# The second expert table's product turned round: 128 tokens held and 512 table columns passing, with sums kept by token and no finishing stage

## The reference, cut to what matters

```python
def one_block(xb):                      # 128 tokens
    ...                                 # eidx: 8 heads x 16 experts of 16384, gate: their softmax
    u = u_tab[eidx]
    act = gelu(einsum('thkd,td->thk', u, xb))
    return einsum('thk,thkd->td', gate * act, v_tab[eidx])
y = rmsnorm(x + out, w_norm_final)
```

## Time and profile before

| what | value |
|---|---|
| median of 3 runs | 3663.56 us (3657.59 to 3664.55) |
| the profiled execution's own time | 3668.83 us |
| its span, first to last instruction | 3667.0 us, mean granted clock 0.984 |
| first matmul of `outputs` | 2554.84 us |
| PE / DVE busy from 3200 to 3400 us | 200.0 / 180.0 of 200 us |
| DMA moved in that stretch | 362 GB/s, share 0.91 |

### The profile page before, as it was taken

One profiled execution on the slowest core, in us unless ns is written; L12 is line 12 of the kernel. 1 busy time (PEld: TensorE's weight loads), 2 busy tenths in 40 slices (PEclk: granted clock), 3 DMA queues, 4 the chain that ended last, 5 costly groups with the idle time before them and its releaser, 6 DMA issues. The chain is left out here.

```text
span 3667.0 us, 50045 instructions
## 1 busy us (share of the span) xinstructions
PE 3528.2 (96%) x19463; PEld 3267.5 (89%) x19463; DVE 2585.5 (71%) x3886; ACT 1314.1 (36%) x1671; POOL 937.1 (26%) x619
## 2 busy tenths in 40 slices
PE   8999999998989999999999999998999999999996
PEld 6877777776867889999999999998999999999996
DVE  4135555553224238999998888886898898998997
ACT  5111134442223223332236767673222222222222
POOL 0000000000000000233333333331555554554552
PEclk9999999999999999999999999999999999999998
DMA  5145343435334244688789999998989999989896
GB/s 204 50 144 172 108 140 128 125 130 185 141 107 162 86 156 160 256 329 333 293 321 364 384 376 375 382 374 343 360 339 372 360 356 377 360 355 370 348 359 243
DMA packets 193659, 965.07 MB, mean 263 GB/s; under 512 B 19697, under 2 KB 67121, under 8 KB 92706
## 3 DMA queue, kind: packets, MB, share of 16 engines
q1 hardware_dynamic: 121010, 516.50, 37.9%
q0 software_dynamic: 61424, 426.27, 29.9%
q10 hardware_dynamic: 11008, 19.26, 1.5%
HBM read 865.58 MB, written 96.37 MB: 262 GB/s over the span
## 5 line engine op out<-in xcount | busy, mean ns | idle before, releaser
L2068 PE MATMUL hidden_hp<-dense_hi,whi 128*128 128x384 f32 x2048 | 699.8, 342 | 6.1 <-PEq L123 6.1
L1836 ACT CAST whi<-raw 128x2048 fp32r<-128x2048 f32 x214 | 410.7, 1919 | 790.5 <-PE outputs_vp L2559 599.9
L2069 PE MATMUL hidden_hp<-dense_lo,whi 128*128 128x384 f32 x2048 | 691.8, 338 | 0.0
L2557 PE MATMUL outputs_vp<-outputs_w_hi,whi 128*128 128x384 f32 x2032 | 679.6, 334 | 3.3 <-DVE wlo L1840 3.1
L2559 PE MATMUL outputs_vp<-outputs_w_hi,wlo 128*128 128x384 f32 x2032 | 678.8, 334 | 0.0
L2558 PE MATMUL outputs_vp<-outputs_w_lo,whi 128*128 128x384 f32 x2032 | 678.7, 334 | 0.0
L2015 POOL DMA_INDIRECT hidden_row<-u_rows,expert_ids x192 | 363.5, 1893 | 1000.4 <-DVE dots L2300 625.4
L1840 DVE TENSOR_TENSOR wlo<-raw,whi 128x2048 fp32r<-128x2048 f32 x214 | 490.2, 2291 | 105.0 <-ACT whi L1836 103.4
L2493 DVE SCALAR_TENSOR_TENSOR accg<-outputs_row,outputs_w_op,accg 128x2048 f32<-128x2048 f32 x192 | 450.7, 2347 | 54.8 <-DMA outputs_row<-v_rows,outputs_id 51.8
L2300 DVE CUSTOM_DVE_ANT_0 hidden_row<-hidden_row,hidden_h_row 128x2048 f32<-128x2048 f32 x192 | 436.0, 2287 | 67.7 <-DMA hidden_row<-u_rows,expert_ids 64.8
L2355 POOL DMA_INDIRECT outputs_row<-v_rows,outputs_id x192 | 325.6, 1696 | 522.3 <-DVE accg L2493 477.8
(11 more groups left out here) (397 smaller groups left out, 5032.6 us busy)
## 6 DMA issues: line engine op xcount, KB each, us to landing
raw<-v_units SPq DMA_DIRECT2D x128, 1024.0 KB
raw<-u_units SPq DMA_DIRECT2D x86, 1024.0 KB
raw<-w_in SPq DMA_DIRECT2D x42, 1024.0 KB, 5.8
hidden_raw<-u_units SPq DMA_DIRECT2D x42, 1024.0 KB
hidden<-hidden_hid SPq DMA_DIRECT2D x128, 192.0 KB
gate_mat<-units_big SPq DMA_DIRECT2D x12, 2048.0 KB, 20.0
units_big<-hidden SPq DMA_DIRECT2D x16, 1536.0 KB
units_big<-gate_mat SPq DMA_DIRECT2D x16, 1536.0 KB
```

What stands on the lines that cost most here:

```text
L1836: self.nc.scalar.copy(self.hi[s][:], self.raw[raw][:]).then_inc(self.hi_done, 1)
L2068: mm(o, un.hi[s][:, x, :], h_hi[:, x, :], start=x == 0, stop=False)
L2069: mm(o, un.hi[s][:, x, :], h_lo[:, x, :], start=False, stop=False)
L2557: mm(o, un.hi[x][:, at, :], W_hi[s][:, e, :], start=e == 0, stop=False)
```

## The change

The product is turned round: the held operand is now a 128-token block of the weights (`W_hi` or `W_lo`, [128 experts x 128 tokens]) and 512 table columns of `hi` or `lo` pass. v_tab's units are packed anew on the host: a unit is now 512 table columns of half a chunk's experts (4 x 128), so two units make one block q of 512 columns. A unit has 3 token tiles x 4 expert blocks x 3 products = 36 matmuls of 512 columns. Results are token by table column, so `acc` is three tiles [128 x 2048] that SP loads with the residual at the start of the stage; DVE adds three 128 x 512 banks every second unit. Six banks are used, two blocks q ahead. Chunk c's first unit needs only the first half of the chunk's `W_lo`. In the last chunk the gathered rows are taken one unit sooner. There is no `finish`: its norm, scaling and stores stand at the end of `outputs`, in a different order, one 1/sqrt for the three dense tiles together, with no transposes and no barrier between.

The core of the diff:

```diff
-                        add(i, s, j, 0)
-                        for x in range(3 * (DS * s + j) // 2, 3 * (DS * s + j + 1) // 2):
+                        for x in rows_of(i, s, j):
                             gathered(i, x)
-                        add(i, s, j, 1)
+            def add(c, q, first=False):
+                for t in range(DTILES):
+                    k = DTILES * (QB * c + q) + t
+                    vec.wait_ge(un.done, NKEYS + DTILES * (DS * c + 2 * q + 1) + t + 1)
+                    if first:
+                        vec.wait_ge(sums_in, 16 * TILES)
...
+                    o = acc[t][:, NB * q:NB * (q + 1)]
+                    v.tensor_tensor(o, o, vp[DTILES * (q % 2) + t][:], ALU.add).then_inc(added, 1)
...
+            for t in range(DTILES):
+                sp.dma_start(acc[t][:], sums[(t + 1) * P:(t + 2) * P, :]).then_inc(sums_in, 16)
             turns(sp, body, T)
...
+                        if j > 0 and j % 2 == 0:
+                            add(c, j // 2 - 1, isinstance(i, int) and i == s == 0)
+                        if j == 0 and not (isinstance(i, int) and i == s == 0):
+                            add(c - 1, QB - 1, isinstance(i, int) and i == 0 and s == 1)
...
+            for c in range(NCH):
+                s = c % 2
+                for j in range(DS):
+                    n, (q, h), x = DS * c + j, divmod(j, 2), j % 2
+                    if j < 2:
+                        pe.wait_ge(w_lo_done, 2 * c + j + 1)
+                    un.ready(pe, NKEYS + n)
+                    for t in range(DTILES):
+                        if h == 0:
+                            wait(pe, added, DTILES * (QB * c + q - 2) + t + 1)
+                        o, at = vp[DTILES * (q % 2) + t], slice(t * P, (t + 1) * P)
+                        for k in range(HC):
+                            e = HC * h + k
+                            mm(o[:], W_hi[s][:, e, at], hi[x][:, k, :], start=e == 0, stop=False)
+                            mm(o[:], W_lo[s][:, e, at], hi[x][:, k, :], start=False, stop=False)
+                            ins = mm(o[:], W_hi[s][:, e, at], lo[x][:, k, :], start=False, stop=e == CH - 1)
+                        ins.then_inc(un.done, 1)
...
-            sp.dma_start(X[:], sums[P:2 * P, :]).then_inc(early, 16)
-            sp.wait_ge(early, 16)
+            sp.wait_ge(gat.row_used, NGATHER - 2)
+            sp.dma_start(norm_w[:], w_row.partition_broadcast(P)).then_inc(norm_in, 16)
```

More of the change, by code:

```diff
@@ L2376, in outputs @@
         Gc = big[1][:, 0:CH * ND].rearrange("p (g e t) -> p g e t", e=CH, t=GT)
+        junk, half, norm_w = big[0][:, 0:D], big[1][0:NSMP, 0:D], gat.row[0]
         W_hi = [a.sb(f"w_hi{s}", [P, CH, ND], F32R) for s in range(2)]
@@ L2447, in body, with square, roots @@
                             weights_hi(2 * i + s + 1, 1 - s, (j - 4) // 2)
+            def square(x, to):
+                R, cols = x.shape[0], x.shape[1]
+                return nc.scalar.activation(junk[0:R, 0:cols], x, ACT.Square, accum_out=to)
+            def roots(n, rows, at):
+                act.wait_ge(meaned, n)
+                nc.scalar.activation(root[0:rows, at], mean[0:rows, at], ACT.Sqrt).then_inc(rooted, 1)
             weights_hi(0, 0, 0)
@@ L2451, in _ @@
             turns(act, body, T)
+            act.wait_ge(w_lo_done, 2 * NCH)
+            act.wait_ge(gat.row_used, NGATHER)
+            square(accg[0][:], ss[:, 0:1]).then_inc(squared, 1)
+            nc.scalar.copy(half, accg[1][NSMP:P, :]).then_inc(moved, 1)
+            roots(1, P, slice(0, 1))
+            act.wait_ge(added, DTILES * (QB * NCH - 1))
+            act.wait_ge(squared, 1)
+            for t in range(DTILES):
+                square(acc[t][:, 0:D - NB], part[:, t:t + 1]).then_inc(parts_done, 1)
+                act.wait_ge(parts_done, t + 1)
+            act.wait_ge(summed, 1)
+            square(accg[1][0:NSMP, :], ss[0:NSMP, 1:2]).then_inc(squared, 1)
+            act.wait_ge(squared, 2)
+            roots(2, NSMP, slice(1, 2))
+            for t in range(DTILES):
+                act.wait_ge(added, DTILES * (QB * NCH - 1) + t + 1)
+                square(acc[t][:, D - NB:D], ss[:, 2 + t:3 + t]).then_inc(squared, 1)
+                act.wait_ge(squared, 3 + t)
+            roots(3, P, slice(2, TILES))
         @block.vector
         def _(vec):
-            v = nc.vector
+            v, d = nc.vector, Steps(vec, dstep)
             def weigh(c, e):
@@ L2470, in weights_lo @@
                                 ALU.subtract).then_inc(w_lo_done, 1)
[L2472 to L2482, removed]
+            def add(c, q, first=False):
+                for t in range(DTILES):
+                    k = DTILES * (QB * c + q) + t
+                    vec.wait_ge(un.done, NKEYS + DTILES * (DS * c + 2 * q + 1) + t + 1)
+                    if first:
+                        vec.wait_ge(sums_in, 16 * TILES)
+                    else:
+                        wait(vec, added, k + 1 - DTILES * QB)
+                    o = acc[t][:, NB * q:NB * (q + 1)]
+                    v.tensor_tensor(o, o, vp[DTILES * (q % 2) + t][:], ALU.add).then_inc(added, 1)
             def gathered(i, j):
@@ L2493, in gathered, with rsqrt, scale @@
                 v.scalar_tensor_tensor(o[:], r[:], w_op[:, j:j + 1], o[:], mult, ALU.add).then_inc(gat.row_used, 1)
+            def rsqrt(n, rows, at):
+                v.tensor_scalar(mean[0:rows, at], ss[0:rows, at], 1.0 / D, EPS, mult, ALU.add).then_inc(meaned, 1)
+                vec.wait_ge(meaned, n)
+                vec.wait_ge(rooted, n)
+                newton_rsqrt(nc, d, rstd[0:rows, at], mean[0:rows, at], root[0:rows, at], tmp[0:rows, at])
+            def scale(x, n):
+                R = x.shape[0]
+                v.scalar_tensor_tensor(x, x, rstd[0:R, n:n + 1], norm_w[0:R, :], mult, mult).then_inc(done, 1)
             def body(i):
@@ L2519, in _ @@
             turns(vec, body, T)
+            vec.wait_ge(squared, 1)
+            rsqrt(1, P, slice(0, 1))
+            vec.wait_ge(norm_in, 16)
+            scale(accg[0][:], 0)
+            vec.wait_ge(moved, 1)
+            v.tensor_tensor(accg[1][0:NSMP, :], accg[1][0:NSMP, :], half, ALU.add).then_inc(summed, 1)
+            add(NCH - 1, QB - 1)
+            vec.wait_ge(squared, 2)
+            rsqrt(2, NSMP, slice(1, 2))
+            scale(accg[1][0:NSMP, :], 1)
+            vec.wait_ge(squared, TILES)
+            vec.wait_ge(parts_done, DTILES)
+            d(v.tensor_tensor(ss[:, 2:TILES], ss[:, 2:TILES], part[:], ALU.add))
+            d.wait()
+            rsqrt(3, P, slice(2, TILES))
+            for t in range(DTILES):
+                scale(acc[t][:], 2 + t)
         @block.tensor
@@ L2523, in _ @@
             mm = nc.tensor.matmul
[L2525 to L2560, removed]
```

128 lines of the change are left out of this document (34 added, 94 removed).

## The result

The change is slower: 3681.3 us, median of five runs (3676.0 to 3691.5), against 3664.6 (3657.6 to 3665.5), a ratio of 1.0049 with a 95% interval of 1.0035 to 1.0063. I had forecast 3640 and a gain of 23 us, and given 0.04 to a kernel slower than 3671. The profiled execution took 3685.5 us, its span is 3683.6.

A forecast was written before the change was run, and what follows sets the result against it. PE's matmul pace was taken as the bound, DVE and DMA a tenth behind. Matmuls -20.0, start +6.7 and +2.5, later stalls +1.5, end -13.9: 23.2 us off the median 3663.56 gives 3640.4; range 3627 to 3655.

The forecast's parts named there:

- The matmuls: PE in mid-stage: 36 matmuls of 0.2267 us make a unit 8.16 us, 0.16 less; -20.0 us over 125 units.
- The start: First chunk: residual loads ahead of units 2 and 3 cost +6.7 us of waiting and +2.5 us of half clock.
- The end: After PE's last matmul: 25.0 us instead of 38.9, so -13.9 us; bounds 21 and 30.
- DVE and the banks: nothing: DVE's list per unit and PE's waits for banks, mid-stage: the moved, wider adds cost no time.
- Later stalls: +1.5 us: PE's waits for `wlo` behind the start: 1.5 us added for the first chunks, none in the steady state.
- L: Lateness of the once-a-chunk load behind the 3 MB of chunk data: 2.4 us steady, 2.8 after the change.
- the limit: The load lateness beyond which PE stalls: 4.1 us before the change, 3.96 after it.
- The bound of +15: Upper bound of the later stalls: 1 us in each of 15 chunks.
- The first rival: Loads take over once a chunk, more gathers ahead of unit 3's load: 3660 (one MB) or 3698 (two); chance 0.07.
- the gathers would come sooner: Mid-stage: DVE, free of waits for PE, takes gathered rows sooner; the -3 us bound of the later stalls.

The follow-up runs named there:

- e2: The changed kernel without the three residual loads at the start of the stage, first chunk's sums being copies; 3675.9 us, 1.0023 to the kernel before.
- e4: The changed kernel with an even unit's three adds behind its gathered row instead of ahead of it; 3659.0 us, 0.9986 to the kernel before.
- b1_late: The kernel before, with each even unit's gathered row taken behind both of the unit's adds; 3677.2 us, 1.0027 to the kernel before.
- e3: The changed kernel with DVE again waiting at the end of each unit's list for PE to finish that unit; 1.0062 to the kernel before.

## Why the prediction was wrong

**The matmuls** were right: 0.2267 us for 512 columns in this stage too, 13.3 ns over the columns, so 20.5 us were given back on PE. The Trainium skill ("TensorE: Matmul & The Clock Gate", Back-to-back issue gap) gives its 2.5 ns for a matmul by itself; the matmuls here, each with a new held block, pay 13.3.

**The start** was near in size: lost 11.4 us in the first chunk against 3.2; e2 without the loads 4.5. I had 6.7 and 2.5 for it. How the waits were split between the third and fourth unit was wrong, so that the sum came out near is in part luck.

**The end** was right within 1.9 us (26.9 for 25.0).

**"DVE and the banks: nothing" is the step that failed.** I had summed DVE's list per unit (9.8 us at most, then 6.5) and asked only whether `wlo` could be late by it. What the moved adds hold up is not DVE's own work but the gathered row behind them, and with it the row buffer, POOL's next gather (whose issue also took 2.6 us instead of 0.96), and how much of the gathers' bytes lands ahead of the fourth unit's load. e4 moved them back and won 22 us. b1_late moved a row back in the old kernel and lost 10 (0.0027 of 3664), there through `W_lo` and the chunk load that waits for it; that path, too, was in the step that I had put at nothing.

**"Later stalls: +1.5 us" then came out as 42.7.** I had let L grow by 0.4 us from the steady 2.4 and found it under 3.96. But 2.4 was the value of one chunk, and near the lowest: counted in the same way, from ACT's idle time less 6.40 us, L in the kernel before is 2.2 to 6.1, 3.3 on the mean of 14 chunks, and rises to 3.9 again in the thirteenth. With 0.4 more the mean is 3.7, only 0.2 under the limit. Measured from PE's release instead, as above, it grew from a mean of 3.5 to 6.2. Even with the rows in the old order it was 5.2 (e4), so the rest of the change, the pace perhaps first, had been priced at too little: 17.5 us where I had allowed 1.5. The bound of +15 was too near; at a 91% share e4's load is 1.7 us later than before (5.2 for 3.5), with units 0.16 us shorter. The first rival named this mechanism and its place, priced one megabyte more ahead of the load at 1.3 us of stall a chunk (3660) and two at 3.8 (3698), and got 0.07. The trace shows 0.7 MB more of gathers, and 3681. The rival, too, started from an L of 2.4 "in every chunk", and it left out what a stall brings with it: half clock in the next unit, 13.6 us of the 47.6.

I also had it that the gathers would come sooner, as DVE no longer waits for PE. e3 put that wait back and nothing changed.

How a stall in one chunk feeds into the next (losses in the change alternate, 0.6, 5.4, 2.8, 6.4, 0.4, 6.0) was not tested. Nor why e4, with the row early, still loses 17.5 us more than the kernel before; what stands is only that a pad of 0.20 us a unit takes 36 us off the change, in part by moving the row.

## What to carry to other kernels

When instructions of an engine change places, ask of each that now comes later what it releases (a buffer, and through it another queue's transfer), and at which other transfer that lands; the engine's own sum doesn't show it. Where the DMA engines are nine tenths full and one load a period is late already, price every change of pace or order by that load's lateness and its limit, and take a bound of several times the simple shift. A load that stands behind a burst can be freed by moving the part of the burst that is needed last behind it.

## What the runs showed of the hardware

Granted clock after short waits of PE in a full stage, from the change: stretches behind waits of 2.1 us (ended 2796.36), 2.5 us (3142.48) and 4.5 us (3212.59),

```profile
2796.00:2802.00 6.00, 5.64 (x18) 4.53 (x19) 6.00 (x8) 1.90 (x1) 0.00 (x0) 0.72 0.79 309
3142.00:3148.00 6.00, 5.52 (x24) 4.58 (x25) 6.00 (x8) 1.91 (x1) 0.00 (x0) 1.00 0.78 284
3212.00:3220.00 8.00, 7.41 (x26) 5.95 (x27) 8.00 (x9) 1.90 (x1) 2.23 (x2) 0.79 0.63 246
```

After 4.5 and after 2.1 us the clock was partly at 1.2 GHz, after 2.5 it stayed at 2.4. Of the ten waits of 2.1 to 4.5 us behind the first chunk seven were followed by the lower level (2.1, 2.4, 3.2, 3.5, 3.9, 4.3 and 4.5 us) and three were not (2.2, 2.2 and 2.5). The seven had 27.3 us at 1.2 GHz behind them, 13.6 us lost. For waits of 2.1 to 2.5 us the length doesn't tell which it will be.

POOL's record of one gather's issue is either about 1 us (0.94 to 1.34) or 1.7 to 4.8. Its mean in this stage went from 1.70 to 1.94 us with the change. What DVE was doing as the issue began (within 0.3 us) goes with it: in the thirteen traces all 1272 long ones began while DVE ran one of its instructions of 1536 or 2048 columns (`wlo`, `W_lo`, a gathered row), as did 109 short ones, and none of the 1115 that began with DVE idle or at a shorter instruction (an add of a bank, `weigh`) was long. That the DVE instruction is what lengthens the issue was not tested by a run, but an order of DVE's list that frees a row buffer just ahead of a long instruction would pay for it, with 1.8 us in the row shown above.
